# Sample keys of the self-attention: turned in 32x32 blocks by VectorE from short-run loads, in place of TensorE turns

## The reference, cut to what matters

```python
k_sel = jnp.where(in_past, cache_k[phys, off], k[bidx, sel_new].astype(cache_k.dtype))
v_sel = jnp.where(in_past, cache_v[phys, off], v[bidx, sel_new].astype(cache_v.dtype))
# sparse_attend, for 16 query heads on 4 key heads:
s = jnp.einsum('bthgd,btnhd->bthgn', qg, k_sel, preferred_element_type=jnp.float32) * (HEAD_DIM ** -0.5)
s = jnp.where((dist >= 0)[:, :, None, None, :], s + bias, -jnp.inf)
p = jax.nn.softmax(s, axis=-1)
o = jnp.einsum('bthgn,btnhd->bthgd', p.astype(v_sel.dtype), v_sel)
```

## Time and profile before

| | |
|---|---|
| median of 3 runs | 2727.49 us (2726.7 to 2729.66) |
| the profiled execution's own time | 2727.95 us |
| its span | 2726.3 us |
| TensorE busy | 98% of the span |
| VectorE, ScalarE, GpSimd busy | 59%, 39%, 8% |

### The profile page before, as it was taken

One profiled execution on the slowest core, in us unless ns is written; L12 is line 12 of the kernel. 1 busy time (PEld: TensorE's weight loads), 2 busy tenths in 40 slices (PEclk: granted clock), 3 DMA queues, 4 the chain that ended last, 5 costly groups with the idle time before them and its releaser, 6 DMA issues.

```text
span 2726.3 us, 49455 instructions
## 1 busy us (share of the span) xinstructions
PE 2678.7 (98%) x20118; PEld 2552.3 (94%) x20118; DVE 1602.2 (59%) x2383; ACT 1074.7 (39%) x1357; POOL 207.3 (8%) x298
## 2 busy tenths in 40 slices
PE   8999999999999999999999999999999999999998
PEld 7999887899999999999989869999999999999997
DVE  5564564476777777677546334485655555653334
ACT  5333454444444444444343334343333233343324
POOL 0102311011111111111100000000000000000000
PEclk9999999999999999999999999999999999999999
DMA  9746656765556556565565794565555555455555
GB/s 267 208 124 160 213 177 209 226 192 157 156 142 165 147 150 162 146 167 141 143 189 140 231 372 112 141 176 143 151 153 143 149 154 144 139 140 151 153 150 146
DMA packets 693465, 458.70 MB, mean 168 GB/s; under 512 B 13646, under 2 KB 661422, under 8 KB 687342
## 3 DMA queue, kind: packets, MB, share of 16 engines
q1 hardware_dynamic: 681008, 414.25, 54.0%
q0 software_dynamic: 8608, 28.06, 3.6%
q10 hardware_dynamic: 3712, 14.35, 1.4%
HBM read 429.91 MB, written 26.72 MB: 167 GB/s over the span
## 4 chain that ended last, share of the span: by engine, by line
PE 93%; DVE 3%; DMA 2%; ACT 1%; issue 1%; SPq 0%; POOL 0%; DVEq 0%; ACTq 0%
PE psum L596 20%; PE psum L601 20%; PE psum L598 20%; PE psum L852 4%; PE psum L1284 4%; PE psum L1285 4%; PE psum L1286 4%; PE psum L857 2%; PE psum L994 1%; PE psum L997 1%; PE psum L990 1%; DMA ring<-in_w_in 1%; PE psum L1165 1%; PE psum L710 1%; PE psum L1006 1%; PE psum L1044 1%
## 5 line engine op out<-in xcount | busy, mean ns | idle before, releaser
L596 PE MATMUL psum<-x_high,w_high 128*128 128x320 f32 x3808 | 1123.9, 311 | 0.5 <-ACT w_high L2022 0.5
L598 PE MATMUL psum<-h_low,w_high 128*128 128x320 f32 x3312 | 974.3, 309 | 0.0
L1331 DVE TENSOR_TENSOR w_low<-ring,w_high 128x2048 fp32r<-128x2048 f32 x292 | 675.9, 2315 | 311.7 <-ACT w_high L2022 311.2
L2022 ACT ACTIVATE w_high<-ring 128x2048 fp32r<-128x2048 f32 x294 | 561.6, 1911 | 677.0 <-PE psum L601 550.1
L596 PEld LDWEIGHTS psum<-x_high,w_high 128*128 128x128 f32 x3808 | 713.1, 188 | 5.8 <-issue 2.4
L598 PEld LDWEIGHTS psum<-h_low,w_high 128*128 128x128 f32 x3312 | 622.0, 188 | 1.6
L601 PE MATMUL psum<-x_high,w_low 128*128 128x320 f32 x3808 | 597.4, 309 | 0.0
L601 PEld LDWEIGHTS psum<-x_high,w_low 128*128 128x128 f32 x3808 | 568.5, 188 | 0.0
L1284 PE MATMUL psum<-y_high,w_down_high 128*128 128x320 f32 x704 | 217.8, 309 | 1.2 <-DVE w_low L1941 1.2
L1286 PE MATMUL psum<-y_high,w_low 128*128 128x320 f32 x704 | 216.3, 307 | 0.0
L1285 PE MATMUL psum<-y_low,w_down_high 128*128 128x320 f32 x704 | 216.2, 307 | 0.0
(11 more groups left out here) (427 smaller groups left out, 2836.4 us busy)
## 6 DMA issues: line engine op xcount, KB each, us to landing
ring<-in_w_in SPq DMA_DIRECT2D x128, 1024.0 KB, 5.8
ring<-in_w_up SPq DMA_DIRECT2D x88, 1024.0 KB, 5.7
ring<-in_w_down SPq DMA_DIRECT2D x64, 704.0 KB, 4.8
ring<-in_w_xk SPq DMA_DIRECT2D x16, 1024.0 KB, 5.9
ring<-in_w_xv SPq DMA_DIRECT2D x16, 1024.0 KB, 5.2
ring<-in_w_out SPq DMA_DIRECT2D x16, 1024.0 KB, 6.0
ring<-in_w_xq SPq DMA_DIRECT2D x16, 1024.0 KB, 6.0
ring<-in_w_xo SPq DMA_DIRECT2D x16, 1024.0 KB, 6.0
```

Of the source, the lines that this page charges most:

```text
L596: mm(out, w_hi[:, j % 2, k, :], x_hi[:, k, :], start=k == 0, stop=False)
L598: mm(out, w_hi[:, j % 2, k, :], lo[:, k, :], start=False, stop=False)
L1331: V.tensor_tensor(w_lo[:, j], ring[:, j], w_hi[:, j % 2].bitcast(FP32), ALU.subtract).then_inc(N.slab_lo, 1)
L2022: F(w_hi[:, j % 2], ring[:, j], ACT.Copy).then_inc(N.slab_hi, 1)
```

## The change

Keys no longer pass through TensorE and ScalarE. VectorE's transpose turns blocks of 32x32 only. So the load itself moves each quarter of a head's elements (index i, 32 elements, 128 bytes) of a page to its own quarter of the partitions, as 4 DMAs of 32 partitions by 16 runs of 128 bytes per page, and one VectorE transpose per page turns the 16 blocks, 128x512 elements, and writes them 4 elements apart. `ktp` and `q_b` get two places each. On VectorE the turn of sample b+1 stands in the iteration of sample b, behind `slab_low` and ahead of `memory_out` and `sample_logits(b)`; it waits there for the loads of sample b+1. TensorE's `page_T`, its waits, and ScalarE's two evacuations are gone. The order of the page loads on POOL stays, except that what releases `k_loads(b)` is now VectorE's turn of sample b-2.

```diff
-        ktp = take(KVH, PAST)
-        q_b = take(2, H, DT)
+        ktp_two = take(2, KVH, PAST)
+        q_b = [take(H, DT), sqbuf[:, 1, P:2 * P].rearrange("p (h t) -> p h t", t=DT)]
...
-            def page_T(b):
-                pe.wait_ge(k_loaded[b % 2], 32 * (b // 2 + 1))
-                pe.wait_ge(N.s_read, H)
-                if b:
-                    pe.wait_ge(N.kt_evac, 2 * b)
-                for i in range(2):
-                    for hh in range(2):
-                        for pg in range(NPG):
-                            h = 2 * i + hh
-                            last = tr(bank(2 + i)[:, (2 * hh + pg) * P:(2 * hh + pg + 1) * P],
-                                      k_page[:, b % 2, pg, h * P:(h + 1) * P], ident)
-                    last.then_inc(N.kt_T, 1)
             def sample_attention(b):
                 pe.wait_ge(N.b_staged, b + 1)
-                pe.wait_ge(N.kt_evac, 2 * b + 2)
+                pe.wait_ge(N.kt_T, b + 1)
...
             for b in range(DB):
-                page_T(b)
...
+            def page_turned(b):
+                dve.wait_ge(k_loaded[b % 2], 64 * NPG * (b // 2 + 1))
+                if b >= 2:
+                    dve.wait_ge(N.s_mm, H + b - 1)
+                ktp = ktp_two[:, b % 2]
+                for pg in range(NPG):
+                    last = V.transpose(ktp[:, :, pg * P:(pg + 1) * P].rearrange("p h (r s) -> p s h r", s=4),
+                                       k_page[:, b % 2, pg].rearrange("p (s h d) -> p s h d", h=KVH, d=32))
+                last.then_inc(N.kt_T, 1)
...
+            page_turned(0)
             for b in range(DB):
                 slab_low(B_MEM + R + H + 1 + b, (b + 1) % R)
+                if b + 1 < DB:
+                    page_turned(b + 1)
...
             def page_evac(b):
                 act.wait_ge(N.s_mm, H + b)
-                F(q_b[:, b % 2], zq[:, :, SEQ + b * DT:SEQ + (b + 1) * DT], ACT.Copy).then_inc(N.b_staged, 1)
-                for i in range(2):
-                    act.wait_ge(N.kt_T, 2 * b + i + 1)
-                    F(ktp[:, 2 * i:2 * i + 2, :], bank(2 + i).rearrange("p (h s) -> p h s", h=2), ACT.Copy)\
-                        .then_inc(N.kt_evac, 1)
+                F(q_b[b % 2], zq[:, :, SEQ + b * DT:SEQ + (b + 1) * DT], ACT.Copy).then_inc(N.b_staged, 1)
...
             def k_loads(b):
-                page_loads(b, k_page, A["cache_k"], k_loaded)
+                for pg in range(NPG):
+                    page = pool.value_load(pages[0:1, NPG * b + pg:NPG * b + pg + 1], min_val=0, max_val=POOL - 1)
+                    for i in range(4):
+                        src = A["cache_k"][0][ds(page, 1)].rearrange("o (r s) h (i d) -> i (o r) (s h) d", s=4, d=32)[i]
+                        pool.dma_start(k_page[32 * i:32 * i + 32, b % 2, pg, :].rearrange("p (x d) -> p x d", d=32), src)\
+                            .then_inc(k_loaded[b % 2], 16)
...
             for b in range(2, DB):
-                pool.wait_ge(N.kt_T, 2 * b - 2)
+                pool.wait_ge(N.kt_T, b - 1)
                 k_loads(b)
                 pool.wait_ge(N.pv_mm, ROWS_AT[b - 2])
                 v_loads(b)
```

More of the change, by code:

```diff
@@ L290, in hybrid_layer @@
         o_rows = sqbuf[:, 1, 0:P]
-        top[0] = CONST["causal"][0]
-        ktp = take(KVH, PAST)
-        q_b = take(2, H, DT)
+        top[0] = CONST["room"][0]
+        ktp_two = take(2, KVH, PAST)
+        q_b = [take(H, DT), sqbuf[:, 1, P:2 * P].rearrange("p (h t) -> p h t", t=DT)]
         bias_s = take(T)
@@ L906, in sample_attention @@
                 for h in range(KVH):
-                    q4 = q_b[:, b % 2, 4 * h:4 * h + 4, :].rearrange("p g t -> p (g t)")
-                    mm(s[32 * h:32 * h + 32, 0:PAST], q4, ktp[:, h, :], start=False, stop=False, skip_group_check=True)
+                    q4 = q_b[b % 2][:, 4 * h:4 * h + 4, :].rearrange("p g t -> p (g t)")
+                    mm(s[32 * h:32 * h + 32, 0:PAST], q4, ktp_two[:, b % 2, h, :], start=False, stop=False, skip_group_check=True)
                     last = mm(s[32 * h:32 * h + 32, PAST:T], q4, kT[:, h, SEQ:T], start=False, stop=True,
@@ L1070, in head @@
                 mm(bank(7)[:, 0:T], ones, osq, start=True, stop=True).then_inc(N.ss_mm, 1)
-            pe.wait_ge(N.kt_evac, 2 * DB)
             by_chunks(B_HG, 1, h_lo, lambda q: pe.wait_ge(rows_loaded[q], 32), lambda q: None, b0=3)
```

## The result

The changed kernel takes 2738.25 us, the median of 5 runs (2737.82 to 2743.45), against 2726.77 us of 5 runs of the kernel before (2724.98 to 2729.66). The ratio is 1.0045, with an interval of 1.0034 to 1.0056: **slower by 12.3 us (9.3 to 15.3)** by that ratio; the two medians themselves lie 11.5 us apart. The forecast was 2731.8 us, in a range of 2720.5 to 2746.0. The profiled execution took 2737.82 us with a span of 2736.3.

What follows compares the result with a forecast made beforehand. The prediction took TensorE to bound the kernel, busy 98% of the span. Its +0.9 us for the chain, net of TensorE's saving, and +3.4 us for the clock gave +4.3 us: 2731.8 us, range 2720.5 to 2746.0.

Steps and rivals of the forecast that it cites:

- the forecast's own case: Samples' stage: a two-iteration chain of 17.5 to 21 us, changing the time by -3 to +10 us; chance 0.56.
- rival B: Key loads: 128-byte runs cost as much as 512-byte ones, 30.2 ns; chain 22.9 us, +18 us, 2745.5 us; chance 0.15.
- TensorE's part: Samples' stage on TensorE: 64 transposes removed, 8 per iteration, saving 6.75 us, all on the path.
- ScalarE's part: ScalarE: 16 copies and their waits go; put at nothing, as ScalarE is busy for half of the stage.
- the early loads: POOL around 295 us: 16 key DMAs for samples 0 and 1 in place of 4; nothing, up to 2 us.
- The chain: Key loads through VectorE's turn and normalisation to TensorE: 18.9 us per two iterations, three times; +0.9 us net.
- The stops: TensorE at `sample_T(b)`, waiting for VectorE's normalisation: about 2.5 us idle in every second iteration.
- The clock: TensorE after a stop: lower granted clock costs about 1.7 us more each, charged for two of three stops, +3.4 us.
- The odd iterations add nothing: Samples' stage: the odd iterations have a chain of the same length running beside the counted one, adding nothing.
- Rival A: Samples' stage: keys land in time, chain 16.1 us, TensorE never stops, whole gain kept, 2720.7 us; chance 0.20.
- Rival C: VectorE's turns: 1.4 us each in place of 0.7, chain 20.3 us, +10.2 us, 2737.7 us; chance 0.09.

Runs made afterwards that it cites:

- a3_both: The changed kernel with POOL issuing keys of sample b+1 ahead of values of b, and VectorE's turn moved behind the normalisation: 2720.51 us, ratio 0.9973 to before.
- c2_memory: The changed kernel with `memory_out` moved ahead of the turn on VectorE, loads in the change's order: 2743.15 us, ratio 1.0047 to before.
- b3_old_short: The kernel before with only the key loads replaced by 8 DMAs of short runs per sample, TensorE still turning: 2751.05 us, ratio 1.0089.
- b2_turn_dense: The changed kernel with the turn's writes dense instead of 4 elements apart, keys left in another order: 2738.62 us, ratio 1.0047 to before.
- a1_k_first: The changed kernel with POOL issuing the keys of sample b+1 ahead of the values of sample b: 2723.08 us, ratio 0.9986 to before.
- a4_long_two: The changed kernel with keys loaded as before, one DMA of 128 rows of 2 KB per page, elements misplaced: 2723.02 us, ratio 0.9982 to before.
- b1_long_eight: The changed kernel with 8 key DMAs per sample kept, each of 32 rows of 2 KB, elements misplaced: 2734.19 us, ratio 1.0026 to before.

## Why the prediction came out as it did

The mechanism was right, and so was its place: VectorE waits ahead of the turn, the normalisation queues behind it, TensorE stops and then runs at half the clock. The sign was right. The size was not: +4.3 us forecast, +12.3 (9.3 to 15.3) measured. Nor were the stops where they were forecast: two long ones, in iterations 3 and 6, in place of three, in 3, 5 and 7. That the stated range holds the result is luck in part: it lies above the -3 to +10 us of the forecast's own case, and inside only because the range takes in rival B, which is false. By its own steps:

- **TensorE's part, 6.75 us saved: right.** `a3_both` has a stage of 65.71 us against 65.1 worked out.
- **ScalarE's part and the early loads at nothing: nothing speaks against it.** ScalarE never waits for a slab in the stage. The 16 early DMAs run from 292.8 to 304.3, and the stage starts no later than before.
- **The chain: 18.9 us forecast, 23.5 measured** (437.66 to 461.15, iterations 2 to 4). In pairs, forecast and measured: to the first key DMA 3.58 and 4.03; issue 4.83 and 5.56; landing with queueing 4.2 and 4.94; two turns 1.4 and 1.83; scores to normalisation 2.41 and 2.49; `sample_T` to the next iteration 2.45 and 4.59. The mis-sized terms: the issue (0.65 us a DMA was about right, 0.69 taken, but two gaps of 0.45 and 0.54 us stand between them, which the sum left out); the landing, in a stretch where the DMA engines are full; and the last, which runs at the lower clock and so was in the clock's term only. With 2.45 us for the last term the chain is 21.4 us, a little beyond the case that the forecast was made for (17.5 to 21).
- **The stops: 7.8 us forecast (3 x 2.6), 11.4 measured**, as 4.26, 0.17, 1.73 and 5.25. VectorE's waits ahead of the turn, named as 2 to 5 us in iterations 2 to 6, were 8.98, 1.62, 6.20, 9.47 and 1.73 us.
- **The clock: 3.4 us forecast for two stops, 8.4 measured. This is the term that was off most**, by 5.0 of the 8 to 9 us that were missing. The price of 1.7 us for a stop was read behind one of 1.9 us, where the next 4 us ran at 0.57. Longer stops by themselves do not explain the rest. In `c2_memory` stops of 4.60, 6.39 and 4.73 us cost 2.4, 1.9 and 2.2 us more; in `b3_old_short` three of 4.93 to 6.42 us cost 5.2 in all (TensorE busy for 77.06 us of the stage, before 71.83), 1.7 each. In the changed kernel a second stop, `memory_out`'s of 1.73 us, falls into the stretch at the lower clock behind the first, and the clock is 0.50 from 456.50 to 468.00, over 11 us: 3.44 x 0.50 + 2.27 x 0.50 + 4.00 x 0.50 + 4.00 x 0.10 = 5.3 us up to 472.00. Behind the single stop of 5.25 us it is 2.89 x 0.50 + 2.10 x 0.50 + 2.90 x 0.25 = 3.2 us. So the sum charged each stop by itself and did not have the one that fell between; and a single stop cost 1.7 to 3.2 us. Why one costs more than another is not shown.
- **"The odd iterations add nothing": wrong twice.** VectorE's `memory_out` also stands behind the turn's wait, which the prediction named in the order but did not follow to TensorE. And that stop moved the chain: the second long stop, in iteration 6, comes from VectorE's wait in iteration 5, an odd one (9.47 us). It took the place of one of the three long ones, as `c2_memory` shows: the stages are 85.36 us with it and 88.24 without. The medians, 2738.25 and 2743.15, point the same way, but the runs overlap.
- **Rival A, keys in time:** false for the change as it is. `a3_both` reaches its 2720.7 with 2720.51, by another order.
- **Rival B, 30.2 ns for a short run:** false, about 12 ns, under the 19 ns from which it would decide. The Trainium skill, "DMA: Bandwidth & Descriptors", section "Specifications", wants 512 B per transfer for the full rate. The trace agrees that 128-byte runs are slower per byte (10.7 against 18.6 bytes per ns); it doesn't bear out what the prediction made of this, that they might take as long as 512-byte ones (12.0 against 30.2 ns).
- **Rival C, turns of 1.4 us:** a turn took 1.09 us, between the 0.7 taken and this, and over the 1 us that the prediction named as a sign of being wrong. It is 0.4 of the 4.6 us by which the chain was longer. That the rival's 2737.7 us is near the measured 2738.25 is luck. The Trainium skill, "SBUF — State Buffer", section "Door 1: The DMA port swizzle (why [64,N] ≈ [32,N])", says that accesses which step to a new 16-byte line are penalised; `b2_turn_dense` agrees, with 1088 against 689 ns.

The profiled executions differ by up to 4.7 us in when the stage starts (421.60 to 426.26), with the same code on TensorE ahead of it. So the span of the changed kernel is only 10.0 us above that of before, while its stage is 13.5 us longer. The medians, 11.5 us apart, lie between. In the same way the profiled executions of `a1_k_first` and `a3_both` took 2720.21 and 2720.56 us, with stages of 67.98 and 65.71 us: a single execution doesn't tell variants apart that lie 2 or 3 us from each other.

## What to carry to other kernels

A wait for something not yet needed, put ahead of urgent work on an in-order engine, turns a late load into a stop of the engine that bounds the kernel: put such a wait behind everything that others wait for, and issue its loads first. Splitting a load into more DMAs costs the time from the first issue to the last, which has to be counted against the slack of the chain, not against the bytes. And a stop has two prices: its length, and the slower clock behind it. The second was 1.7 to 3.2 us for a single stop of 4.6 to 6.4 us here, and 5.3 us where another stop fell into the slow stretch; so what lies just behind a stop has to be followed too.

## What the runs showed of the hardware

- **The clock behind a stop.** Behind a stop of 2.53 us (`a1_k_first`, ended at 458.25) it stays at 1.00, and as well behind one of 2.45 us (`a4_long_two`). Behind 2.77 us (`b2_turn_dense`, ended at 454.83) it is 0.59, behind 2.74 us (`b1_long_eight`) 0.71. Behind the stops of 4.26 and 5.25 us of the changed kernel it is 0.50. A stop of 1.9 us ahead of the stage left it at 1.00 in the changed kernel, and in the kernel before it fell behind it. So the same short stop doesn't always have the same price, and these rows give no length from which the clock falls. The windows behind the stops, first of `a1_k_first`, then of `b2_turn_dense` (columns as above):

```profile
458.00:460.00 2.00, 1.75 (x8) 1.44 (x9) 1.24 (x4) 0.85 (x4) 1.15 (x2) 1.00 1.16 236
```

```profile
454.80:459.00 4.20, 4.03 (x38) 2.24 (x38) 2.60 (x3) 3.22 (x7) 1.98 (x4) 0.59 1.08 299
```

- **Short runs on POOL's queue** cost about 12 ns of engine time per 128 bytes: more than the 7.5 ns that their bytes would take at the rate of the slabs' 512-byte runs, a good deal less than the 30.2 ns of such a run.
- **VectorE's transpose** of 128x512 fp32 elements takes 689 ns with dense writes, as long as a copy of that shape out of PSUM (692 ns), and 1088 with writes 16 bytes apart.
- **The DMA engines can run at 0.96** through a stage without holding up TensorE (`a3_both`), with slabs landing 8.2 us after issue, 2.8 us later than before.
